# Paged-cache attention of a decoder step: cached keys turned in 32x32 blocks by VectorE, their scores on 4x4 tiles of TensorE, and the query path put ahead of the prompt's memory keys and values

## What is computed

```python
# both groups, c_q = rmsnorm(cq), c_kv = rmsnorm(ckv)
q = (c_q @ w_uq).reshape(B, S, 8, 128 + 64)
q_rope = rope(q[..., 128:], pos)
q_lat = jnp.einsum('bshn,rhn->bshr', q[..., :128], w_uk)

# sample group: 8 sequences, 2048 cached keys each in pages of 128
keys_lat = concat([cache_lat[page_table], c_kv])       # 128 wide
keys_rope = concat([cache_rope[page_table], k_rope])   # 64 wide
s = (q_lat . keys_lat + q_rope . keys_rope) * ATTN_SCALE
p = softmax(s);  o_lat = p . keys_lat

# prompt's memory, needed only by the cross attention near the end
mem_k, mem_v = rmsnorm(mem) @ w_mk, rmsnorm(mem) @ w_mv   # 256 x 512 each
...
h = h + moe(rmsnorm(h, g_ffn), ...)                    # 32 experts
```

## Time and profile before

| | |
|---|---|
| median of 3 runs | 1527.2 us (1524.54 to 1527.66) |
| profiled execution | 1534.05 us, span 1532.2 us |
| granted TensorE clock, mean | 0.981 |
| busy share of the span | PE 94%, DVE 24%, ACT 18%, POOL 5% |
| chain that ended last | PE 81%, DMA 12%, DVE 3%, ACT 2% |

### The profile page before, as it was taken

How to read it: one execution, slowest core, us unless ns; L and a number is a source line. 1 busy time by engine, 2 the same in 40 slices (tenths; PEclk the granted TensorE clock), 3 DMA queues, 4 the chain that set the end, 5 groups by cost and what they waited for, 6 DMA issues and landing times.

```text
span 1532.2 us, 18708 instructions
## 1 busy us (share of the span) xinstructions
PE 1441.7 (94%) x7647; PEld 785.0 (51%) x7647; DVE 373.3 (24%) x950; ACT 270.4 (18%) x579; POOL 81.4 (5%) x104
## 2 busy tenths in 40 slices
PE   7978998989999888999999999999999999999997
PEld 5755776758888664433443443433433443433433
DVE  2243234221023432211221221221221221221212
ACT  3144423032112230001001101101001001101102
POOL 0152020100010100000000000000000000000000
PEclk9999999889999997999999999999999999999999
DMA  9464353472372765999999999999899999999993
GB/s 332 157 242 156 110 171 111 145 260 103 119 274 110 275 253 217 391 429 428 428 429 427 429 427 430 428 428 398 364 431 426 429 427 428 429 427 429 427 428 163
DMA packets 62438, 494.72 MB, mean 323 GB/s; under 512 B 5263, under 2 KB 6472, under 8 KB 37816
## 3 DMA queue, kind: packets, MB, share of 16 engines
q1 hardware_dynamic: 50904, 453.92, 71.6%
q0 software_dynamic: 11488, 40.15, 7.8%
HBM read 487.00 MB, written 7.05 MB: 322 GB/s over the span
## 4 chain that ended last, share of the span: by engine, by line
PE 81%; DMA 12%; DVE 3%; ACT 2%; issue 1%; another core or an unknown queue 1%; SPq 0%; DVEq 0%; ACTq 0%
PE bank L1142 22%; PE bank L664 16%; PE bank L1169 12%; DMA ring<-in_w_gate_up 6%; DMA arena<-in_w_down 5%; PE bank L1125 5%; PE bank L620 4%; PE bank L1181 4%; PE bank L636 3%; PE bank L1128 2%; PE bank L1149 2%; PE bank L688 1%; PE bank L1155 1%; PE bank L907 1%; PE bank L1011 1%
## 5 line engine op out<-in xcount | busy, mean ns | idle before, releaser
L1142 PE MATMUL bank<-ring,arena 128*64 128x512 f32 x1536 | 345.0, 598 | 4.3 <-DMA ring<-in_w_gate_up 4.2
L1169 PE MATMUL bank<-arena 128*64 128x512 f32 x976 | 217.1, 595 | 9.8 <-DMA arena<-in_w_down 9.8
L1142 PEld LDWEIGHTS bank<-ring,arena 128*64 128x64 f32 x1536 | 104.5, 137 | 223.5 <-issue 211.8
L664 PE MATMUL bank<-arena,ring 128*128 128x264 f32 x896 | 211.1, 396 | 0.0
L664 PEld LDWEIGHTS bank<-arena,ring 128*128 128x128 f32 x896 | 171.6, 194 | 36.3 <-issue 6.2
L1169 PEld LDWEIGHTS bank<-arena 128*64 128x64 f32 x976 | 67.9, 137 | 144.0 <-issue 124.5
L2121 DVE TENSOR_TENSOR resid<-resid,bank 128x264 f32<-128x264 f32 x128 | 54.9, 429 | 340.4 <-PE bank L1181 338.9
L1142 PE MATMUL bank<-arena 128*64 128x512 f32 x512 | 115.3, 592 | 0.0
L2126 DVE TENSOR_SCALAR arena<-bank 128x512 f32<-128x512 f32 x32 | 22.0, 687 | 306.8 <-PE bank L1142 306.8
L1125 PE MATMUL bank<-arena 128*128 128x128 f32 x544 | 82.3, 297 | 10.7 <-DVE resid L2121 8.5
L1283 ACT ACTIVATE arena<-bank 128x264 f32<-128x264 f32 (+6 forms) x131 | 48.9, 382 | 200.3 <-PE bank L664 139.5
(11 more groups left out here) (289 smaller groups left out, 1145.2 us busy)
## 6 DMA issues: line engine op xcount, KB each, us to landing
ring<-in_w_gate_up SPq DMA_DIRECT2D x96, 2048.0 KB, 22.5
arena<-in_w_down SPq DMA_DIRECT2D x61, 2048.0 KB, 18.6
arena<-in_w_gate_up SPq DMA_DIRECT2D x32, 2048.0 KB, 26.8
ring<-in_w_in SPq DMA_DIRECT2D x10, 2048.0 KB, 8.8
ring<-in_w_down SPq DMA_DIRECT2D x3, 2048.0 KB, 41.3
out<-arena POOLq DMA_DIRECT2D x10, 512.0 KB, 5.1
arena<-in_state_gla POOLq DMA_DIRECT2D x8, 512.0 KB, 4.7
ring<-in_w_o_mla SPq DMA_DIRECT2D x2, 2048.0 KB, 7.8
```

The source lines that it names most:

```text
L664: mm = nc.tensor.matmul(lin_bank(name)[0:m, 0:width], w(ring_name, nk, cols)[:, k, a:a + m], rhs[:, k, 0:width], start=(k == 0), stop=(k = ...
L1142: mm = nc.tensor.matmul(B[i // 2][CAP * (i % 2):CAP * (i % 2) + CAP, :], xg[:, k, CAP * e:CAP * e + CAP], slot(n)[:, a:a + 512], start=Fal ...
L1169: mm = nc.tensor.matmul(B[4][CAP * half:CAP * half + CAP, :], hT[:, c, CAP * (k // 4):CAP * (k // 4) + CAP], slot(j)[:, a:a + 512], start= ...
```

## The change

The memory keys `mk1` to `mk3` and the memory values leave the place before the queries. `mk0` stays, `mk1` comes after the new product `qb`, `mk2`, `mk3`, `mv0` and `mv1` stand between the score rounds. `uk` and `norm(3)` come ahead of the turns of the memory tokens. `w_uq` is loaded before `w_mk`.

The key tiles are no longer turned by PE. DVE turns each with two block transposes (1024 and 512 columns), which turn every 32x32 block in itself. The four strips of 32 partitions then hold different keys, so a score matmul has 32 rows, 32 columns and 256 keys, and the 128 + 64 contracted numbers come as six chunks `c` of 32: 96 matmuls per round, sequence j in column group j, strip a in row group a with a bank of its own. The queries have to stand on all four strips: `qb` copies them there by a product with stacked identity blocks (`copies`), and DVE brings them into `q_blocks`. POOL's first gather waits for `m7` to be turned, where it waited for `mv1`, and its later ones for DVE's turns. The query pairs' rotation takes another place in memory, `own` is computed with a product over elementwise products, and the stores of the memory keys and values move behind the gathers.

```diff
-LIN = (["cq0", "cq1", "ckv", "kr", "rotk"] + [f"mk{h}" for h in range(4)] + ["mv0", "mv1"]
+LIN = (["cq0", "cq1", "ckv", "kr", "rotk", "mk0"]
        + [f"qn{h}" for h in range(8)] + [f"qr{j}" for j in range(4)] + [f"rot{j}" for j in range(4)]
-       + [f"ql{h}" for h in range(8)] + ["own0", "own1", "rep0", "rep1"] + EARLY[0:1] + ["ga"] + EARLY[1:2] + [f"la{h}" for h in range(4)]
+       + [f"ql{h}" for h in range(8)] + ["qb", "mk1", "own0", "own1", "rep0", "rep1", "mk2", "mk3", "mv0", "mv1"]
...
-RING_SLOT = [0, 1, 2, 3, 0, 1, 2, 0, 1, 2, 0, 3, 1, 2, 0, 3, 1, 2, 0, 3, 1, 2, 0]
+RING_SLOT = [0, 3, 1, 2, 0, 1, 2, 0, 1, 2, 0, 3, 1, 2, 0, 3, 1, 2, 0, 3, 1, 2, 0]
...
+        copies = view(1024, 512)
+        q_blocks = past[:, 1, :].rearrange("p (g n) -> p g n", g=2)[:, :, 0:768].rearrange("p g (c j k) -> p g c j k", c=6, j=4)
+        PAST_BANKS = [B[4], B[5], B[6], B[7]]
...
             pool.wait_ge(S("idx"), 2)
-            lin_full(pool, "mv1")
-            for n in range(4):
+            pool.wait_ge(S("turn_full"), TI["m7"] + 1)
+            for n in range(16):
+                if n >= 4:
+                    pool.wait_ge(S("keys_turned"), n - 3)
                 gather_past(n, True)
...
-            pe.wait_ge(S("q_sample"), 5)
+            lin_done(pe, "ql7")
+            pe.wait_ge(S("q_roped"), 1)
+            pe.wait_ge(S("q_copies"), 1)
+            open_bank("qb")
+            for c in range(4):
+                nc.tensor.matmul(lin_bank("qb")[:, 64 * c:64 * c + 64], copies[:, P * c:P * c + P], big4[:, :, PROMPT:T], start=True, stop=True)
+                mm = nc.tensor.matmul(lin_bank("qb")[:, 256 + 32 * c:288 + 32 * c], copies[:, P * c:P * c + P], q_pairs[:, :, PROMPT:T],
+                                      start=True, stop=True)
+            mm.then_inc(S("product_full"), 1)
+            project(["mk1"], "mk", 8, 512, memT, NMEM, first=P)
...
+            def past_scores(q):
+
+                pe.wait_ge(S("keys_turned"), 4 * q + 4)
+                if q:
+                    pe.wait_ge(S("past_copied"), 4 * q)
+                for c in range(6):
                     for j in range(4):
-                        mm = nc.tensor.matmul(out[32 * j:32 * j + 32, :].rearrange("p (a i k) -> p a i k", a=2, i=2)[:, :, i, :],
-                                              q_rope_wide[:, i, 4 * (n // 4) + j, :], KTr[j][:, 256 * c:256 * c + 256],
-                                              start=False, stop=(i == 1))
+                        for a in range(4):
+                            rows = slice(32 * a, 32 * a + 32)
+                            if c < 4:
+                                keys = KTl[j][rows, :].rearrange("p (t c k) -> p c t k", t=8, c=4)[:, c]
+                            else:
+                                keys = KTr[j][rows, :].rearrange("p (t c k) -> p c t k", t=8, c=2)[:, c - 4]
+                            mm = nc.tensor.matmul(PAST_BANKS[a][32 * j:32 * j + 32, 0:256].rearrange("p (t k) -> p t k", t=8),
+                                                  q_blocks[rows, q // 2, c, j, :], keys, start=(c == 0), stop=(c == 5))
                 mm.then_inc(S("past_scores"), 1)
...
+            past_scores(0)
+            project(["mk2", "mk3"], "mk", 8, 512, memT, NMEM, first=2 * P)
+            past_scores(1)
+            lin_done(pe, "mk3")
+            pe.wait_ge(S("past_copied"), 8)
+            for tt in range(2):
+                turn(f"mkt{tt}", [(128 * h, memk[:, h, tt * P:(tt + 1) * P]) for h in range(4)])
...
+            memory_values_of_prompt(0)
+            turned(pe, "mkt0")
+            turned(pe, "mkt1")
+            past_scores(2)
+            pe.wait_ge(S("past_copied"), 12)
+            turn_probs(0)
+            memory_values_of_prompt(1)
+            turned(pe, "P0_2")
+            turned(pe, "P0_3")
+            past_scores(3)
             normed_done(pe, 1)
             early(0)
...
+            def turn_keys(n):
+
+                j = n % 4
+                dve.wait_ge(S("past_scores"), n // 4) if n >= 4 else None
+                dve.wait_ge(S(f"lat{j}"), 16 * (n // 4 + 1))
+                V.transpose(KTl[j], flat(lat[j]))
+                dve.wait_ge(S(f"rope{j}"), 16 * (n // 4 + 1))
+                V.transpose(KTr[j], rop[j]).then_inc(S("keys_turned"), 1)
```

More of the change, by code:

```diff
@@ L283, in lin_full, with normed_done @@
             eng.wait_ge(S("product_full"), LI[name] + 1)
-        def normed_done(eng, k, c=None):
-            eng.wait_ge(S("normed"), sum(NORM_CHUNKS[j] for j in range(1, k)) + (NORM_CHUNKS[k] if c is None else c + 1))
+        def normed_done(eng, k):
+            order = list(NORM_CHUNKS)
+            eng.wait_ge(S("normed"), sum(NORM_CHUNKS[j] for j in order[:order.index(k) + 1]))
         def squares_before(k):
@@ L570, in _ @@
                 gather_past(n, False)
+                if n == 3:
+                    for tt in range(2):
+                        turned(pool, f"mkt{tt}")
+                        pool.dma_start(o_memk_p[0, 0, tt * P:(tt + 1) * P].rearrange("p h d -> p (h d)"), mk_tok[tt]).then_inc(S("mem_k_stored"), 16)
+                    lin_done(pool, "mv1")
+                    pool.dma_start(o_memv_p[0, 0].rearrange("(t p) h d -> p t (h d)", p=P), memv).then_inc(S("stored"), 16)
             pool.wait_ge(S("gla_qk"), 1)
@@ L627, in turn @@
                 i = TI[name]
-                if i == KEY_TURNS[2]:
-                    lin_done(pe, "own1")
-                earlier = [j for j in range(i) if turn_bank_number(j) == turn_bank_number(i)]
-                if earlier:
-                    pe.wait_ge(turn_sem(name), earlier[-1] // 2 + 1)
+                if i >= 2:
+                    pe.wait_ge(turn_sem(name), i // 2)
                 for at, src in parts:
@@ L701, in _ @@
             input_product("kr", C_KR, ROPE)
+            pe.wait_ge(S("uk_loaded"), 16)
+            for g in range(2):
+                turn(f"uk{g}", [(128 * j, wuk[:, (4 * g + j) * 128:(4 * g + j + 1) * 128]) for j in range(4)])
+            pe.wait_ge(S("pages"), 1)
+            pe.wait_ge(S("const_loaded"), 16)
+            nc.tensor.matmul(SCORE_BANK[:, 0:8], con("spread", 16), pages[0:16, 8:16], start=True, stop=True).then_inc(S("page_rows"), 1)
+            norm(3, squares, 2, T)
             pe.wait_ge(S("mem_scaled"), 1)
@@ L733, in _ @@
                 mm.then_inc(S("product_full"), 1)
-            lin_done(pe, "mk3")
-            for tt in range(2):
-                turn(f"mkt{tt}", [(128 * h, memk[:, h, tt * P:(tt + 1) * P]) for h in range(4)])
             normed_done(pe, 4)
@@ L1378, in probs_out, with past_scores_out @@
                         turn_out(f"P{g}_{c}", [(past[:, g, 512 * c:512 * c + 512], P, (0, 512))])
-            for q in range(4):
-                for j in range(4):
-                    keys_out(4 * q + j)
-                    if q == 2 and j == 0:
-                        past_exp(0)
-                for c in range(2):
-                    act.wait_ge(S("past_scores"), 2 * q + c + 1)
-                    a = 1024 * (q % 2) + 512 * c
-                    nc.scalar.copy(past[:, q // 2, a:a + 512], SCORE_BANKS[c][:]).then_inc(S("past_copied"), 1)
-                if q == 2:
-                    probs_out(0)
+            def past_scores_out(q):
+                act.wait_ge(S("past_scores"), q + 1)
+                for a in range(4):
+                    dst = past[:, q // 2, 1024 * (q % 2):1024 * (q % 2) + 1024].rearrange("p (t a k) -> p a t k", t=8, a=4)[:, a]
+                    nc.scalar.copy(dst, PAST_BANKS[a][:, 0:256].rearrange("p (t k) -> p t k", t=8)).then_inc(S("past_copied"), 1)
+            past_scores_out(0)
+            for h in (2, 3):
+                out(f"mk{h}", memk[:, h, :], width=NMEM)
+            past_scores_out(1)
+            turn_out("mkt1", [(mk_tok[1], P, (0, 512))])
+            past_exp(0)
+            out("mv0", memv[:, 0, :], width=512)
+            past_scores_out(2)
+            probs_out(0)
+            out("mv1", memv[:, 1, :], width=512)
+            past_scores_out(3)
             def early(*numbers):
@@ L1740, in _ @@
             input_out("kr", krT)
+            turn_out("uk0", [(ukT[:, 0:512], P, (0, 512))])
+            dve.wait_ge(S("page_rows"), 1)
+            for i in range(2):
+                V.tensor_scalar(idx[:, i, :], SCORE_BANK[:, 0:8], con("within")[:, i:i + 1], 2.0, ALU.add, ALU.mult).then_inc(S("idx"), 1)
             for c in range(0, KC, 2):
@@ new lines, in _ @@
+            V.tensor_tensor(own_lat[:, :, 0:8], big4[:, :, PROMPT:T].rearrange("p h b -> p b h"), bc(ckvT[:, PROMPT:T, None], [P, 8, 8]), ALU.mult)\
+                .then_inc(S("q_sample"), 1)
+            for odd in range(2):
+                half = slice(64 * odd, 64 * odd + 64)
+                V.tensor_tensor(own_rope[half, :, odd:8:2], q_pairs[half, :, PROMPT:T].rearrange("p j b -> p b j"),
+                                bc(krT[half, PROMPT:T, None], [64, 8, 4]), ALU.mult).then_inc(S("q_sample"), 1)
```

226 lines of the change are left out of this document (87 added, 139 removed).

## The result

| | before | after |
|---|---|---|
| median | 1524.54 us (1523.17 to 1527.66, 5 runs) | 1514.12 us (1512.05 to 1517.26, 5 runs) |
| profiled execution, span | 1534.05, 1532.2 us | 1514.12, 1512.3 us |

The ratio is 0.9944, with a 95% interval of 0.9924 to 0.9963: faster by 10.4 us, where 29 were forecast. (The median before is of five executions here, where 1527.2 was of three.) `gv0` starts at 127.20 us, not at 115.0.

What follows compares the result with a forecast made beforehand. PE was taken as the bound, 94% busy, with waits in the score rounds. 71.7 + 12.0 + 31.3 put `gv0` at 115.0 instead of 144.1 us; 29 off the median gave 1498 us, range 1490 to 1514.

Steps and rivals of the forecast that it cites:

- `gv0` before the change: Start of the first product after the score rounds in the old kernel, read from one trace as 144.1 us.
- round 0 begins: Start of the first score round, where PE's and DVE's paths from `qb` were to tie, at 71.7 us.
- four score rounds: Score matmuls of all four rounds, at 3.0 us each, 12.0 us together.
- three gaps: Time between the four score rounds, filled with key tiles and moved memory products, 31.3 us together.
- Query pairs and round 0: Ahead of the rounds: query pairs ready at 64.0 us, `qb` done at 66.4, first round at 71.7.
- A key tile on DVE, 1.22 + 0.68: Two block transposes per key tile on DVE, 1.9 us, estimated from float32 operations of one element a step.
- The rival of the double price: Block transposes on DVE cost 3.8 us a tile, +27 us together, ending at 1525 us; chance 8%.
- Gaps 9.1, 10.0 and 12.2: Times in us between rounds 0 and 1, 1 and 2, 2 and 3, from DVE's and PE's work there.
- The score round: Each round's 192 records take 3.0 us, sixteen tiles at once: 12 steps of 0.216 us plus start and tail.
- The subtraction from the median: The 29 us won before `gv0` taken whole from the median, giving 1498 us; the range's upper end carries 7 us.
- the first, with issue at a price: Score rounds of 5.2 to 5.9 us, from tiles not sixteen at once or 30 ns issue: 1507 to 1510 us; 22%.
- Row groups: In score rounds, neighbours differing in rows queue behind each other: 20.7 us a round, +71, 1569 us; chance 5%.

Runs made afterwards that it cites:

- before_again: The kernel before the change, unedited, profiled a second time: 1527.5 us in one execution, `gv0` at 137.58 us.
- tiles_twice: The changed kernel with every block transpose done twice in a row: ratio 1.0134 to the kernel before, 1543.97 us.
- halved_columns: The changed kernel with each score matmul cut into two of 128 keys, 384 records a round: ratio 1.0152 to the kernel before, 1548.03 us.
- scores_twice: The changed kernel with each round's 96 score matmuls issued twice: ratio 1.0148 to the kernel before, 1546.73 us.
- four_chunks: The changed kernel with four of the six score chunks, 64 matmuls of 256 columns a round: ratio 0.9915 to the kernel before.
- load_held: The changed kernel with the `gq` weight load waiting for the end of score round 1: ratio 0.9920 to the kernel before, 1510.1 us.
- quiet_round: As load_held, with POOL's gathers of tiles 8 to 11 also waiting for the end of score round 1: ratio 0.9947 to the kernel before.
- strip_outside: The changed kernel with the score matmuls' inner loops swapped, strip outside and sequence inside: ratio 0.9917 to the kernel before, 1512.70 us.
- wide_chunks: The changed kernel with 48 score matmuls of 512 columns a round in place of 96 of 256: ratio 0.9858 to the kernel before, 1512.70 us.
- after_again: The changed kernel, unedited, run and profiled once more: ratio 0.9926 to the kernel before.
- mended: As load_held, with `mk1` ahead of `qb`, tile 2 turned before the query-block copies, `mv1` ahead of the first probabilities' turns: 0.9931, 1513.48 us.

## Why the prediction was wrong, step by step

The sign, the mechanism of the gain and its place were right; the size was not, and 1514.12 lies just above the range. Against `before_again` the stretch won 10.4 of the 29.1 us forecast. The missing 18.7:

| step of the sum | forecast | measured | missing |
|---|---|---|---|
| `gv0` before the change | 144.1 | 137.6 | 6.5 |
| round 0 begins | 71.7 | 72.05 | 0.35 |
| four score rounds | 12.0 | 4.65 + 9.0 + 4.5 + 4.3 = 22.45 | 10.4 |
| three gaps | 31.3 | 8.2 + 11.3 + 13.2 = 32.7 | 1.4 |

- **Query pairs and round 0.** Pairs were to be ready at 64.0; `qb` in fact starts at 63.5. `mk1` took 5.18 in place of 3.45: PE had idled 1.53 us ahead of `qb`, and the clock was 0.75 in the stretch. `qb` (1.98 in place of 2.4), `own` and `rep` were cheaper. That round 0 came at 72.05 all the same is luck: these errors cancel.
- **A key tile on DVE, 1.22 + 0.68.** Measured 1.22 + 0.67, as estimated from products of two operands. The rival of the double price falls. The Trainium skill's 311 ns for 128 columns, in "VectorE: DVE Perf Modes", "The three transpose paths", taken as a rate would be 3.7 us a tile, an estimate; the trace has 1.9, so a rate it is not here.
- **Gaps 9.1, 10.0 and 12.2.** Measured 8.2, 11.3 and 13.2. The last two carry half clock behind the hole and in the turns of the probabilities (1.94 and 1.97 us for eight turns, granted clock 0.50). DVE closed only the first gap, where PE waited 1.11 us for it. In the other two its last tile was done at 103.2 and 120.6, while PE was at `mv0` and `mv1` until 105.3 and 122.9: in the second, which the forecast gave to DVE by 0.1 us, PE's own half clock decided. `tiles_twice` shows that DVE had no more than these 2 us to spare.
- **The score round, "I take 3.0, as each axis works by itself".** This is the step that failed. Tiles do multiply: round 1 opens with 33 records in 0.50 us, near the forecast's 16 in 0.216. But then PE takes no record faster than about 20 ns, and a round is at least 4.0; without the hole the four were 4.65, 5.0, 4.5 and 4.3 = 18.4 in place of 12.0, so this floor cost 6.4 of the 10.4 us. The prediction had it on the table as "some 12 to 25 ns" and chose near its lower end (3.0 us is 15.6 ns a record), as if only the columns counted. `halved_columns`, `scores_twice` and `four_chunks` show the price of the records.
- **Code loading** was in no step. It has the other 4.0 us of the rounds, and the half clock behind the hole. A round uses up one and a half packets of code in 4 us, and the next packet is late behind gathers and weights. The packets' times and `load_held` and `quiet_round` show it.
- **The subtraction from the median.** The prediction named the 6.58, the 2.84 and the half clock behind as of unknown standing, and yet subtracted 29 whole. `before_again` has neither of the two stretches, and its half clock lies elsewhere. This is 6.5 of the missing 18.7, as much as the price of the records.
- **The rivals.** Nearest was the first, with issue at a price; it had 5.2 to 5.9 us a round from the wrong row (30 ns, L871), and 1507 to 1510. The Trainium skill's 25 ns in "TensorE: Matmul & The Clock Gate", "Back-to-back issue gap", would have made 4.8 us, an estimate; the traces have 4.0 to 5.0 without holes, so counted by records the figure is high as a floor (19.7 ns here), but nearer than the choice. Row groups don't get in each other's way (`strip_outside`). The gathers were not late for DVE; what they and the weights held up was PE's code.
- **From `gv0` on 1388 us as before.** 1385.1 in the profiled run, and 1381.5 (`load_held`) to 1393.4 (`wide_chunks`) over the kernels here. Where a piece of this was looked at (the outer products above), the clock made the difference.

What stays open: what the trickle is and why the same program has it in one execution and not in another, what of the 20 ns is the matmul's and what its weight load's, and how the reorder alone would do with the keys still turned by PE; it wasn't tried.

## What to carry to other kernels

Cutting a matmul into row and column tiles trades PE's columns for instructions: count the records, at some 20 ns each, before counting columns, and then count the code, which arrives by the same DMA engines as the data. Here a packet held 128 records, 2.8 us of such a round, and in round 2 of `halved_columns` the packets came 3.7 us apart (119.1, 122.8, 126.5). The gain of a change that fills PE's waits with moved work is bounded by the waits of a typical execution, so read a second trace of the kernel before sizing it. Here the new rounds paid only together with the moved memory products: without the move they lose 0.85%. What the move wins without them is not shown.

## What the hardware showed that was not expected

- **Instruction fetches are visible and can stop PE.** They come in packets of 16 KB (36 in the span), one for 128 records (768 records more brought 6 packets more). With the DMA engines full PE stood 4.01 us, with them empty 0.59 us, and it went on 2.3 to 2.7 us after the packet.
- **A record of a 32x32 tile costs 20 to 23 ns** with 128 or with 256 columns, and 35 ns with 512 (96 in 3.40 us). The first 33 of round 1, after PE's idle 1.11 us, took 0.50 us, 15 ns each.
- **Float32 block transposes on DVE** run at one column a step of 1.08 ns, (1222 - 669)/512, with 0.12 us fixed.
- **The clock differs between executions of one program.** It was 0.50, the lower level, right behind PE's idle 4.01 us, and 1.00 behind its idle 1.11 us. The 56 records of the sample outer products took 11.37 us at a mean clock of 1.00 in the changed kernel, 14.70 us at 0.77 in `after_again`, the same program, and 13.06 us at 0.87 in `mended`.
